# Expert outputs weighed at their eviction and added in DRAM by an accumulating scatter, in place of a weighing tail

## The reference

```
    x = x + gate1 * (merged @ w_o)
    h = _rmsnorm(x, g_ffn) * (1 + scale2) + shift2
    return x + gate2 * _hier_moe(h, w_rg, b_rg, w_re, b_re, w_gate_e, w_up_e, w_down_e)
...
    w_top = jax.nn.softmax(top_v, axis=-1) * p_top
...
    return jnp.einsum('btef,efd->btd', jax.nn.silu(a) * b * combine[..., None], w_down_e)
```

## Time and profile before

| | |
|---|---|
| median of three runs | 912.7 us |
| profiled execution, device time | 909.47 us |
| its span, first to last instruction | 907.6 us |
| mean granted TensorE clock, share of full speed | 0.917 |
| PE, DVE, ACT, POOL busy, share of the span | 82%, 32%, 20%, 18% |
| moved by DMA | 194.59 MB |
| 64 loads of gate and up halves, 32 of down | 1 MB each, landing after 20.4 us in the median |

### The profile page before, as it was taken

The page is one execution under the profiler, slowest core; times in us unless marked ns, Lnnn a source line. Parts: engine busy times, 40 slices in busy tenths (PEclk is TensorE's granted clock), DMA queues, the critical chain, the costliest instruction groups (busy, mean ns, idle before and its releaser), DMA issues.

```text
span 907.6 us, 12945 instructions
## 1 busy us (share of the span) xinstructions
PE 742.8 (82%) x5111; PEld 570.5 (63%) x5111; DVE 294.5 (32%) x621; ACT 182.7 (20%) x325; POOL 159.5 (18%) x249
## 2 busy tenths in 40 slices
PE   0799999999999899899998998339988888887800
PEld 0398988798887779799994444225544554554400
DVE  1552231367656231222324323541211111111156
ACT  1442222333333024122110101101111011011031
POOL 1710003102200000000000100222332323232144
PEclk9999999999999589999999999559999899989955
DMA  9644659662141045422108701307999999999452
GB/s 305 267 163 165 253 192 333 241 205 96 48 163 36 13 162 168 140 71 70 47 25 320 314 23 51 135 19 272 416 417 420 418 419 418 419 417 418 205 216 94
DMA packets 36454, 194.59 MB, mean 214 GB/s; under 512 B 6882, under 2 KB 7082, under 8 KB 19240
## 3 DMA queue, kind: packets, MB, share of 16 engines
q1 hardware_dynamic: 27504, 171.24, 48.1%
q0 software_dynamic: 8384, 21.83, 6.9%
q10 hardware_dynamic: 520, 0.87, 0.3%
HBM read 186.91 MB, written 15.27 MB: 223 GB/s over the span
## 4 chain that ended last, share of the span: by engine, by line
PE 64%; DMA 19%; DVE 6%; issue 4%; ACT 2%; SPq 2%; POOL 1%; POOLq 0%; DVEq 0%; ACTq 0%
PE bank L1480 28%; DMA arena<-in_w_gate_up 14%; PE bank L1678 8%; PE bank L1642 5%; PE bank L1697 3%; PE bank L1606 3%; PE bank L1514 3%; DMA arena_b<-in_w_ada 3%; PE bank L1563 3%; PE bank L1583 2%; PE bank L1419 2%; PE bank L1603 2%; DMA arena<-in_w_in 1%; PE bank L1533 1%; DMA arena<-y_scratch 1%
## 5 line engine op out<-in xcount | busy, mean ns | idle before, releaser
L1480 PE MATMUL bank<-h_parts,w_parts 128*128 128x260 f32 x2160 | 273.7, 286 | 1.0 <-DVE w_parts L980 0.8
L1480 PEld LDWEIGHTS bank<-h_parts,w_parts 128*128 128x128 f32 x2160 | 263.5, 189 | 15.4 <-issue 13.2
L1678 PE MATMUL bank<-arena,arena_b 128*64 128x256 f32 x1024 | 136.2, 425 | 34.6 <-issue 27.6
L1678 PEld LDWEIGHTS bank<-arena,arena_b 128*64 128x64 f32 x1024 | 89.0, 153 | 72.9 <-issue 41.1
L980 DVE TENSOR_TENSOR w_parts<-arena,w_parts 128x1024 fp32r<-128x1024 f32 x46 | 56.2, 1223 | 73.0 <-ACT w_parts L807 72.8
L1321 DVE TENSOR_TENSOR arena_b<-bank,arena_b 128x128 f32<-128x128 f32 x32 | 9.3, 292 | 183.2 <-ACT arena_b L909 183.2
L1697 PE MATMUL bank<-arena,arena_b 128*64 128x512 f32 x256 | 60.9, 593 | 0.8 <-DVE arena_b L1327 0.8
L733 POOL DMA_INDIRECT y_scratch<-arena_b x32 | 32.6, 1018 | 155.3 <-DVE arena_b L1333 75.8
L1642 PE MATMUL bank<-arena,arena_b 128*128 128x512 f32 x128 | 56.2, 596 | 0.0
L807 ACT ACTIVATE w_parts<-arena 128x1024 fp32r<-128x1024 f32 x46 | 48.4, 1053 | 34.3 <-DMA arena<-in_w_in 27.3
L587 POOL TENSOR_TENSOR arena_b<-arena_b 128x1 f32<-128x1 f32 (+1 forms) x15 | 12.0, 801 | 211.8 <-DVE arena_b L1192 179.1
(11 more groups left out here) (266 smaller groups left out, 735.3 us busy)
## 6 DMA issues: line engine op xcount, KB each, us to landing
arena<-in_w_gate_up SPq DMA_DIRECT2D x64, 1024.0 KB, 20.4
arena<-in_w_down SPq DMA_DIRECT2D x32, 1024.0 KB, 20.4
arena<-in_w_in SPq DMA_DIRECT2D x46, 512.0 KB, 3.9
arena<-in_w_ada SPq DMA_DIRECT2D x22, 1024.0 KB, 7.0
arena_b<-in_x_prompt SPq DMA_DIRECT2D x8, 512.0 KB, 12.8
arena<-in_w_o SPq DMA_DIRECT2D x2, 2048.0 KB, 8.0
arena<-y_scratch SPq DMA_DIRECT2D x4, 1024.0 KB, 9.6
arena_b<-q_scratch POOLq DMA_DIRECT2D x3, 1024.0 KB, 5.7
```

The costliest lines, as they stand in the source:

```text
L1480: ins = pe.matmul(ps[s][:, 0:HALF], w_parts[:, n % 2, wp, k], h_parts[:, hp, k, s * HALF:(s + 1) * HALF], start=(k == 0 and hp == 1), stop ...
L1678: ins = pe.matmul(ps[2 + b][R * hh:R * hh + R, 0:2 * P], hTe[:, b, c * P + jj * R:c * P + jj * R + R], w_gu[slot][:, 4 * jj + c, :, hh * P ...
```

## The change

Each row's weight and gate are applied when an expert's result leaves PSUM, and the scatter adds the product to a row of `y_d` that already holds x.

- `y_d` has 2T half rows in place of 4T. SP stores tiles 0 to 3 of x into it (three stores between the loads of weight slots 2 and 3, the fourth behind slot 3); POOL stores zeros into the 8 sample rows, whose gate differs by row.
- The gather and scatter lists become one. In place of the second list, the one-hot matmul brings the weight of each slot's row. `per_slot` holds for each slot: is it a prompt row, is it a sample row, its weight.
- For each expert DVE copies three columns out of `per_slot` and builds a 128x512 factor (gate2 for prompt rows, 1 for sample rows) in the place of x tile 0; the eviction is then PSUM times weight times factor.
- The scatter has `compute_op=ALU.add`. Two experts of one row add to the same place, so scatter e waits on POOL until scatter e - 1 has landed.
- In the tail SP loads the rows of `y_d` straight to x. Tiles 0 to 3 are only squared, normed and stored; the sample tile is first multiplied with its gate and added to x. All five results have a buffer of their own. The order is 0, 4, 1, 2, 3.

```diff
-        y_d = nc.dram_tensor("y_scratch", [4 * T, D // 2], F32).ap()
+        y_d = nc.dram_tensor("y_scratch", [2 * T, D // 2], F32).ap()
...
+        TAIL = (0, 4, 1, 2, 3)
...
+            y2 = y_d.rearrange("(t j) d -> t (j d)", j=2)
             for j in range(EUN):
                 if j == EUN - 1:
+                    for i in range(3):
+                        sp.wait_ge(s_x2, i + 2)
+                        sp.dma_start(y2[i * P:(i + 1) * P], x[:, i]).then_inc(s_y0, 16)
                     sp.wait_ge(s_wom, 10)
                 load_gate_up(j, j)
                 load_down(j, j)
+            sp.wait_ge(s_x2, 5)
+            sp.dma_start(y2[3 * P:4 * P], x[:, 3]).then_inc(s_y0, 16)
...
             sp.wait_ge(s_moe, 1)
-            y4 = y_d.rearrange("(t k j) d -> t k (j d)", k=2, j=2)
-            for i in RB:
-                if i < 4:
-                    sp.dma_start(yk[:, i], y4[i * P:(i + 1) * P]).then_inc(s_yk[i], 16)
-                else:
-                    sp.dma_start(yk_s, y4[TP:T]).then_inc(s_yk[i], 16)
+            sp.dma_start(y_s, y2[TP:T]).then_inc(s_yk[4], 16)
+            for i in range(4):
+                sp.dma_start(x[:, i], y2[i * P:(i + 1) * P]).then_inc(s_yk[i], 16)
...
+            pool.wait_ge(s_smo, 1)
+            pool.memset(zero, 0.0).then_inc(s_zero, 1)
+            pool.wait_ge(s_zero, 1)
+            pool.dma_start(y_d[2 * TP:2 * T].rearrange("(b j) (i d) -> b (j i) d", j=2, i=2), zero).then_inc(s_yz, 16)
...
             def scatter(e, j, ix):
-                pool.tensor_copy(si[:, j:j + 1], lists[:, 0, ix]).then_inc(s_sx, 1)
+                pool.tensor_copy(si[:, j:j + 1], lists[:, ix]).then_inc(s_sx, 1)
                 apart(s_sx, e + 1)
                 apart(s_ye, e + 1)
-                b = j % 2
+                apart(s_sc, 16 * e)
                 pool.indirect_dma_start(out=y_d, out_offset=bass.IndirectOffsetOnAxis(ap=si[:, j:j + 1], axis=0),
-                                        in_=ys[:, b], in_offset=None,
-                                        bounds_check=last_written, oob_is_err=False).then_inc(s_sc[b], 16)
+                                        in_=ys[:, j % 2], in_offset=None, bounds_check=last_row, oob_is_err=False,
+                                        compute_op=ALU.add).then_inc(s_sc, 16)
...
             for e in range(AHEAD):
                 gather(e, e, column(e))
+            pool.wait_ge(s_y0, 16 * 4)
+            pool.wait_ge(s_yz, 16)
...
-            for n, i in enumerate(RB):
-                r = rows[i]
-                md = mod_p if i < 4 else mod_s
-                pool.wait_ge(s_mix, n + 1)
-                pool.tensor_tensor(mix[0:r, n % 2], mix[0:r, n % 2], md[0:r, 3], ALU.mult).then_inc(s_mixg, 1)
-                if n:
-                    inverse_root(10 + n - 1, RB[n - 1])
-            inverse_root(14, RB[4])
+            for n, i in enumerate(TAIL):
+                inverse_root(10 + n, i)
...
+            for n, i in enumerate(TAIL):
                 r = rows[i]
-                pair = yk[:, i] if i < 4 else yk_s
-                act.wait_ge(s_yk[i], 16)
-                act.activation(pair[0:r, 0], pair[0:r, 0], ACT.Copy, scale=wk[0:r, 0, i:i + 1]).then_inc(s_w0, 1)
...
+                act.wait_ge(*((s_yk[i], 16) if i < 4 else (s_x3, 1)))
+                act.activation(res[0:r, i], x[0:r, i], ACT.Square, accum_out=ssq[0:r, i:i + 1]).then_inc(s_sq3, 1)
...
-            for k in range(2):
-                link(dve.tensor_scalar(code[:, k], tok1, 2.0, float(k - 1), ALU.mult, ALU.add))
-                link(dve.tensor_tensor(code[:, k], code[:, k], valid, ALU.mult))
...
-            link(dve.tensor_copy(lists_f, ps[3][:, 0:2 * NTILE]))
...
+            dve.tensor_copy(per_slot[:, 2], ps[3][:, NTILE:2 * NTILE])
+            dve.tensor_scalar(per_slot[:, 0], lists_f, 2.0 * TP - 0.5, None, ALU.is_lt)
+            dve.tensor_scalar(per_slot[:, 1], lists_f, 2.0 * TP - 0.5, None, ALU.is_gt)
+            link(dve.tensor_copy(mod_p[R:P, 3, 0:512], mod_p[R:P, 3, 512:D]))
+            gate_h = mod_p[:, 3, 0:512]
...
+            def factor_of(e, j, ix):
+
                 b = j % 2
+                dve.tensor_copy(slot_col[:, b], per_slot[:, :, ix].rearrange("p a o -> p (a o)")).then_inc(s_col, 1)
+                dve.wait_ge(s_col, e + 1)
+                dve.tensor_scalar(factor[:, b], gate_h, slot_col[:, b, 0:1], slot_col[:, b, 1:2], ALU.mult, ALU.add
+                                  ).then_inc(s_fct, 1)
+
+            def down_of(e, j):
+                b = j % 2
+                dve.wait_ge(s_fct, e + 1)
                 dve.wait_ge(s_y, e + 1)
-                at_least(dve, s_sc[b], written)
-                dve.tensor_copy(ys[:, b], ps[5 + b][:]).then_inc(s_ye, 1)
+                at_least(dve, s_sc, 16 * e - 16)
+                dve.scalar_tensor_tensor(out=ys[:, b], in0=ps[5 + b][:], scalar=slot_col[:, b, 2:3], in1=factor[:, b],
+                                         op0=ALU.mult, op1=ALU.mult).then_inc(s_ye, 1)
...
+            dve.wait_ge(s_yk[4], 16)
+            link(dve.tensor_tensor(y_s, y_s, mod_s[:, 3], ALU.mult))
+            dve.tensor_tensor(x[0:TS, 4], x[0:TS, 4], y_s, ALU.add).then_inc(s_x3, 1)
...
+            dve.wait_ge(s_gf, 16)
             for n in range(5):
...
+                mean_square(n)
+                normed(n)
```

More of the change, by code:

```diff
@@ L179, in hybrid_step @@
         actT = cube(region("QK", qk_work + 2 * D + 4 * P, 2 * P), 2)
[L181 to L182 removed]
+        factor = cube(region("X", 0, D), 2)
+        y_s = region("SPLIT", 8 * D, D, TS)
         gfin_b = region("SPLIT", 10 * D, D)
[L184 to L185 removed]
+        res = cube(region("SPLIT", 0, 5 * D), 5)
         small = [0]
@@ L213, in hybrid_step @@
         wk = cube(take(2 * 5), 2)
+        zero = scS[:, :, 0:256]
         rt = [0]
@@ L260, in hybrid_step @@
         tilek = cube(rtake(10), 2)
-        code = cube(rtake(10), 2)
         t10 = cube(rtake(10), 2)
@@ L374, in hybrid_step @@
         s_ye = sem("s_ye")
-        s_sc = [sem(f"s_sc{i}") for i in range(2)]
+        s_sc = sem("s_sc")
+        s_col = sem("s_col")
+        s_fct = sem("s_fct")
+        s_zero = sem("s_zero")
+        s_y0 = sem("s_y0")
+        s_yz = sem("s_yz")
         s_go = sem("s_go")
@@ L385, in hybrid_step @@
         s_res = sem("s_res")
-        s_out = [sem(f"s_out{i}") for i in range(2)]
+        s_out = sem("s_out")
         s_dve = sem("s_dve")
@@ L928, in _ @@
                     silu_of(o + NE, 0)
-            def weigh(n):
-                i = RB[n]
+            for n, i in enumerate(TAIL):
                 r = rows[i]
-                pair = yk[:, i] if i < 4 else yk_s
-                act.wait_ge(s_yk[i], 16)
-                act.activation(pair[0:r, 0], pair[0:r, 0], ACT.Copy, scale=wk[0:r, 0, i:i + 1]).then_inc(s_w0, 1)
-            weigh(0)
-            weigh(1)
-            for n, i in enumerate(RB):
-                r = rows[i]
-                if n + 2 < 5:
-                    weigh(n + 2)
-                act.wait_ge(s_x3, n + 1)
-                act.activation(mix[0:r, n % 2], x[0:r, i], ACT.Square, accum_out=ssq[0:r, i:i + 1]).then_inc(s_sq3, 1)
+                act.wait_ge(*((s_yk[i], 16) if i < 4 else (s_x3, 1)))
+                act.activation(res[0:r, i], x[0:r, i], ACT.Square, accum_out=ssq[0:r, i:i + 1]).then_inc(s_sq3, 1)
         @block.vector
@@ L1254, in _ @@
             dve.engine_nop().then_inc(s_rw, 1)
-            for k in range(2):
-                link(dve.tensor_scalar(code[:, k], tok1, 2.0, float(k - 1), ALU.mult, ALU.add))
-                link(dve.tensor_tensor(code[:, k], code[:, k], valid, ALU.mult))
+            dve.wait_ge(s_ra, 2)
+            link(dve.tensor_reduce(ptop, gexp, AX.X, ALU.add))
+            link(dve.scalar_tensor_tensor(out=wk[:, 0], in0=wk[:, 1], scalar=1.0, in1=ptop, op0=ALU.add,
+                                          op1=ALU.mult))
+            link(dve.reciprocal(wk[:, 0], wk[:, 0]))
+            link(dve.tensor_tensor(wk[:, 1], wk[:, 1], wk[:, 0], ALU.mult))
             dve.wait_ge(s_rp, 1)
@@ L1351, in _ @@
                     act_turned(o + NE, 0)
-                    down_of(o + NE, 0, 16 * o + 16 * (NE // 2))
-            def mixed(n):
-                i = RB[n]
-                r = rows[i]
-                pair = yk[:, i] if i < 4 else yk_s
-                dve.wait_ge(s_w0, n + 1)
-                if n >= 2:
-                    dve.wait_ge(s_sq3, n - 1)
-                dve.scalar_tensor_tensor(out=mix[0:r, n % 2], in0=pair[0:r, 1], scalar=wk[0:r, 1, i:i + 1],
-                                         in1=pair[0:r, 0], op0=ALU.mult, op1=ALU.add).then_inc(s_mix, 1)
-            def summed(n):
-                i = RB[n]
-                r = rows[i]
-                dve.wait_ge(s_mixg, n + 1)
-                dve.tensor_tensor(x[0:r, i], x[0:r, i], mix[0:r, n % 2], ALU.add).then_inc(s_x3, 1)
+                    factor_of(o + NE, 0, column(o + NE))
+                    down_of(o + NE, 0)
```

(5 more changed lines are left out.)

72 lines of the change are left out of this document (26 added, 46 removed).

## The result

The changed kernel takes 943.09 us (median of four runs, 935.92 to 947.56); the kernel before, on the same chip, 914.43 us (four runs, 912.27 to 917.54). The ratio is 1.0303, with an interval of 1.0255 to 1.0352: slower by 3%, outside the predicted range and on the other side of the forecast. The profiled execution of after is the shortest of its four, 935.92 us with a span of 934.1 us; it stands against the 907.6 us span of before.

What follows compares the result with a forecast made beforehand. Bound: DMA bytes moved in the expert stage, then a tail chain over four engines. 909.47 - 19.8 - 0.45 + 10.4 + 1.5 = 901.1 us for the profiled execution, 904.3 for runs; range 893 to 930.

Steps and rivals of the forecast that it cites:

- Part 3: Expert stage: each scatter waits for the previous landing; a step of 8.2 us fits the 8.24 us left.
- Rival (b): Expert stage: the chain of scatters becomes the bound, from a step of 8.52 us; 926 us, chance 0.18.
- Part 1: Tail after the last scatter landing: last norm after 16.1 us instead of 35.9, a gain of 19.8 us.
- Part 2: Expert stage: adding rows also fetch old values, 88 ns a row on saturated DMA engines, 10.4 us more.
- (a): Expert stage: the add is hidden, the old value being fetched in parallel; 897 us, chance 0.15.
- (c): Expert stage: an adding row costs three or four times a plain one; 919 us, chance 0.13.
- Part 4: Other edits (stores of x, zero fill, factor, routing): little or no cost, 0.45 us gained in routing.
- Rival (d): Tail: less is gained, through slow powers or a late start of the chain; 909 us, chance 0.10.
- The end of the stage: Last scatters: scatter 30 holds back scatter 31, which lands later; 1.5 us for both, 2.2 at most.
- The sign: Whole kernel: faster (under 908.1 us) 0.58, within 4.6 us of no change 0.20, slower 0.22.

Runs made afterwards that it cites:

- b_chain: Kernel before, where a plain scatter also waits for the landing of the previous one; 914.7 us, ratio 1.0005.
- a_inter: Changed kernel with experts in the order 0, 8, 16, 24, 1, ..., a scatter waiting only for the one four back; 910.95 us, ratio 0.9938.
- b_add_chain: Kernel before with both adding scatters and the wait for the previous landing; 962.53 us, ratio 1.053.
- b_add: Kernel before with the scatter made an adding one onto zeros, no wait added; 927.69 us, ratio 1.0136.
- c1: Kernel before with gate2 applied at the eviction, plain scatters, and DVE adding weighted rows onto x in the tail; 903.92 us, ratio 0.9873.
- a_plain: Changed kernel whose scatter writes plainly instead of adding but keeps the wait; 896.52 us, ratio 0.979.

## Why the prediction was wrong

**Part 3, the added wait: here it failed.** Its form was right. A step is the landing plus 0.8 us: b_chain has 7.4 to 7.6, after 9.0 + 0.8 = 9.8 against 9.85 measured. The term that was mis-sized is the landing of an adding scatter: 7.4 us in the sum, 9.0 measured. "8.2 fits, by a hair" stood on a landing of 7.4 us, made of 6.7 for a plain scatter and 0.35 + 0.1 + 0.25 on top. Measured is 9.0, 2.3 on top. Of these up to 0.6 is POOL's issue, which grew from 1.02 to 1.60 us (the landing is counted from its start): I had seen that it might double, and took 0.25 of it for no better reason than that the middle was wanted. The other 1.7 stand where I had put 0.45 for rows and source. That term was worked out as engine time, 88 ns a row, when what a row costs in a landing beside full queues is waiting: with 4 KB packets the same rows land 1.5 us earlier. The text itself said that 0.1 us of landing costs up to 2.8 us, and by that rule 1.6 us more are 45 us over the forecast. Measured are less: stage and last landing were forecast at 237.1 + 2.35 + 10.4 + 1.5 = 251.4 us and took 282.1 + 3.8 = 285.9, so 34.5 over it, since the last five steps are short. (The table's +45.0 us is against before, and 10.4 us of it were forecast.) A margin of 0.04 us on a term known to 1 us is a coin's toss, and should have had more of the chance than 0.18.

**Rival (b) was the right mechanism, priced too low.** It said that the chain becomes the bound from a step of 8.52 us, and that a step would be 9 to 10 where a row takes two turns; the step was 9.85. It was then taken down to 8.8 to 9.4, on the ground that the landing shortens when the loads no longer fill the engines. That second step failed: at a share of 0.92 to 0.95 the landing was still 9.0 us, against 9.3 beside 0.98 to 1.03, and only when the loads ran out did it fall (6.0, then 3.7 to 4.8). Its own numbers also gave 920 to 937 us, of which it took 926. With the steps as measured, 26 of 9.85 us and then five that take 26.1 together (before 34.8, from 828.5 to 863.25 us), (b) gives 904.3 + 34.5 = 939 us for the median of the runs, against 943.09, and 901.1 + 34.5 = 935.6 for the profiled execution, against 935.92. That the landing hardly varies with the experts' row counts spoke against two turns a row, and in a sense still does, as the 4 KB runs show; what an adding row has in place of a plain one's is two packets, 97 ns more of engine time and a longer issue, and no run separates these as causes of the longer landing.

**Part 1, the tail.** Right: 19.9 us gained for 19.8, norms 2.0 us apart, the power at 0.55 us. The start of the chain was 0.7 us late, and the steps made most of it up.

**Part 2, the added DRAM work.** Right in size: 12.6 us in the runs of the add alone (7 to 18 by the interval; 12.7 in the stage) for 10.4, 186 ns a row instead of 2 x 88. Rivals (a) and (c) fall with it. The Trainium skill ("Collectives: The Full Stack", section "The bandwidth ceiling: the fold count and why AG ≠ RS ≠ AR") says of the reduce step of a collective that it issues one descriptor for each of its two sources and so runs at half the rate of a copy, 1.93 as measured there. For an adding scatter, of which it doesn't speak, the traces agree, with two packets a row and 2.1 times the engine time. In after itself the term doesn't show as time, since DMA isn't full there on average.

**Part 4.** Right as far as the runs tell: with plain writes the change takes 896.52 us, 18.5 less than before, where parts 1 and 4 alone had 20.25. Routing, forecast 0.45 us shorter, ended where it was (scatter 0 at 626.09 against 626.11): the operations on the lists take 0.97 us instead of 1.35, but start 0.46 us later. Rival (d) falls.

**The end of the stage.** Here the sum had 1.5 us, though its own working gives more: scatter 31 held until 864.9 to 865.1 instead of 863.25, and 0.1 to 0.4 us more of landing, is 1.75 to 2.25. The two parts measured are 1.6 us (4.49 us from scatter 30 to 31 for 2.91) and 1.45 us of landing (3.8 for 2.35), 3.0 together. The landing is again what was priced too low, by the same misjudgement as in part 3.

**The sign.** The two terms that were well known, -19.8 and +10.4, gave "faster" a good chance, and a_inter shows them: 910.95 us, 0.6% under before (0.2 to 1.0% by its interval), at the edge of what can be told from no change. The sign was decided by the one that was least known.

## What to carry to other kernels

- In these runs a wait for the landing of the previous DMA costs nothing as long as landing + 0.8 us fits into what the stage leaves for a step. Beyond that it costs the excess times the steps, less what is won back once the loads have ended: b_add_chain against b_add, 26 steps of 9.90 us for 8.21 are 44 us, the last five win back 10 (26.6 for 36.4), and the stages differ by 34. Price the landing under the load that will stand beside it and with the operation that will be used; here an adding scatter landed after 3.7 us in a quiet DMA and 9.0 beside the weight loads.
- Two changes that are cheap alone (0 and 12.6 us) cost 47.5 together here, as both use up the same slack. Where a forecast says "fits by a hair", test the combination, or make the slack: an order in which neighbours don't conflict, so that the wait goes four back instead of one, took back 32 us with the same work.
- Before moving work into DMA, see how much of the gain is to be had without it: weighing onto x on DVE (c1) got 11 us of the tail's 20 at no cost elsewhere, and ended 7 us under the best kernel with adds.

## What the runs showed of the hardware

- The adding form of the indirect scatter occupies POOL for 1.60 us against 1.02, for 128 slots with 65 filled in the mean and one index column, loaded or not (1.60 too with the light loads).
- An adding row counts as two packets in the software queue and costs 186 ns of engine time for 89.
- The median landing of a scatter beside loads of 8 KB packets is 6.7 us plain, 9.0 adding; beside 4 KB packets 5.9 and 7.5; the last scatters, after the loads, have 2.35 to 3.5 plain and 3.7 to 4.8 adding. For the adding one it hardly falls when the DMA share does: 9.3 us at 0.98 to 1.03, 9.0 at a mean of 0.94.
- The same bytes in 4 KB rows in place of 8 KB lengthened the stage of before by 7.0 us of 237.
- The profiles differ by 9 us in the time before scatter 0 (625.4 to 634.5 us), also between kernels that are the same up to there: 626.1 us in after and 634.5 in a_plain. The length of the stage in question tells more than the end of one profile.
